# A decoder block on one core: when rests of weights are taken, in which order GLA's and FOX's first blocks run, and how the second norm is interleaved

## The chip, the cores and the metric

The kernel runs on 1 core of one Trainium2 chip. The metric is the device time of one execution in microseconds (us), the median of several runs. Lower is better.

## What is computed

One layer of a decoder block, 256 tokens by 2048 channels, all in float32:

```python
mod = silu(c) @ w_ada + b_ada                      # shift1, scale1, gate1, shift2, scale2, gate2
h = rms_norm(x, g_norm1) * (1 + scale1) + shift1
proj = h @ w_in                                    # 16416 columns: gq gk gv gg ga_low | fq fk fv f_logit | gate_a gate_b
o_a = rms_norm(gla(gq, gk, gv, log_a)) * silu(gg)  # gated linear attention, 4 heads
o_b = forgetting_attention(fq, fk, fv, log_f)      # FOX: causal softmax with a forget bias, 16 heads
merged = sig(gate_a) * (o_a @ w_proj_gla) + sig(gate_b) * (o_b @ w_proj_fox)
x = x + gate1 * (merged @ w_out)
h2 = rms_norm(x, g_norm2) * (1 + scale2) + shift2
x = x + gate2 * (relu(h2 @ w_ff1) ** 2 @ w_ff2)
out = rms_norm(x)
```

## The kernel before, in words

**Blocks and units.** Each product with a weight is cut into blocks of 512 output columns (a name such as `("fq", 1)`: FOX's queries, second block), and each block into 8 units of 256 rows of the weight. `NAME` (line 45) is the order of the blocks, and unit g is the g-th unit of the program: 0 to 23 the head (`gg`, `gv`, `fq`, first blocks, taken in two halves of h's channels), 24 to 119 the FOX blocks, 120 to 191 GLA's, 192 to 319 the gates and projections, 320 to 351 the output product, 352 to 607 the feed-forward. `("qk", 0)` holds GLA's first 256 query columns and first 256 key columns side by side, so its units are loaded by two DMAs with rows of 1 KB each; all other units are one DMA with rows of 2 KB. Both move 512 KB.

**Precision.** A product is computed in three passes of the float32r format: each weight unit is split into a top part (`whi`, by ScalarE, `hi(g)`, line 716) and a rest (`wlo` = weight minus top, by VectorE, `lo(g)`, line 1195). `h` is split in the same way (`hT`). `token_unit` (line 1801 and on, the matmul's line is 1817) runs the 12 matmuls of a unit and first waits for `lo(g)`. There are 4 buffers for the split weights, so `hi(g)` waits until TensorE has finished unit g-4, and 5 buffers for the loaded ones (`raw`), shared by the units and the rides.

**Rides.** The vector `mod` is also computed on the way. Its parts that the first norm needs come in 64 pieces of 512 KB (`first`, loop over `PIECES`), each multiplied into an accumulator by VectorE (line 1167); the others ride along with the units: `RIDE_AT` says at which unit g a ride (a 512 KB load of `w_ada`, rows of 4 KB, and one VectorE multiply-add, line 1313) is done, and `MOD_AT` at which unit TensorE sums a finished one. `ride_all` (line 162) writes these places; its last lines step g by 5, 2 or 3 units. The loads of units and rides go in one order (`STREAM`) through SyncE's queue, each after the buffer five places earlier is free.

**The ramp.** While the pieces run, SyncE loads unit g at piece `LOAD_AT[g]`, VectorE takes its rest by piece `SPLIT`, and TensorE runs it by piece `RUN`. At piece 32, VectorE also makes h's second half of channels (`norm1_chunk(1)`). After piece 63, `sum_first(3)` on TensorE, `mod_first(3)` on VectorE and `shift_hi`, `shift_lo` complete h. The head and units 24 and 25 run during the ramp; from unit 26 the loop over FOX follows, where u counts the 24 units of one `it`.

**The turn.** FOX needs queries and keys transposed. ScalarE copies a finished block from PSUM to `fqk_tok` (`stage`, line 739), TensorE transposes it with 8 small matmuls (`turn`, line 1801), and ScalarE copies the result out (`take_turned`, line 747). For `("fq", 0)`, ScalarE stages at u = 5, after `hi` of the unit 3 ahead, and TensorE turns at u = 7, ahead of unit 31. For `("qk", 0)`, they stand at u = 8 (stage), 10 (turn) and 11; for `("fk", 0)` at 16, 18 and 19. All engines run their instructions strictly in the order in which they are written. `small` (16 + 16 narrow columns of `w_in`) is loaded by GpSimd's queue in 16 small DMAs from unit 21 on, and multiplied at u = 11 (`small_cols`, lines 1856 and 1858).

**The second norm** begins in the first units of the feed-forward, which run on the not yet shifted h2 (`obT`) for the first up block. Per channel tile k: `norm2_apply` (VectorE, line 1588) scales xT, `norm2_hi` (ScalarE, line 1043) makes its top, `norm2_lo` (VectorE, line 1594) its rest. VectorE's round u does `lo(g+3)`, then apply for two tiles, then `norm2_lo` for the two tiles of the round before; ScalarE's round u does `hi(g+3)`, then `norm2_hi` for two tiles. At u = 8 VectorE finishes the first up block (`ff_first`, lines 1642 and 1646), TensorE turns it at u = 11, and ScalarE and VectorE split the result at u = 12.

Of the kernel before, what the change touches and what calls it, by code (L numbers as in the profile page):

```python
# [13 lines left out]
KT = D // P  # L14
# [24 lines left out]
HEAD = [("gg", 0), ("gv", 0), ("fq", 0)]  # L39
FOX = [("qk", 0), ("fk", 0), ("fv", 0)] + [(what, it) for it in range(1, 4) for what in ("fq", "fk", "fv")]  # L40
GLA = [(what, it) for it in range(1, 4) for what in ("qk", "gg", "gv")]
# [63 lines left out]
LOAD_AT = [13, 14, 15] + [17 + 7 * _i // 4 for _i in range(9)] + [32] + [33 + 2 * _i for _i in range(1, 12)] + [57, 59, 61]  # L105
FOX_EARLY = 2
LOADED, SPLIT, RUN = [0] * PIECES, [0] * PIECES, [0] * PIECES
for _g, _p in enumerate(LOAD_AT):
    for _r in range(_p, PIECES):
        LOADED[_r] = _g + 1  # L110
    for _r in range(max(_p + 2, KT), PIECES):
        SPLIT[_r] = _g + 1
    if _g < G_FOX + FOX_EARLY:
        for _r in range(max(LOAD_AT[_g | 1] + 3, KT + 1), PIECES):
            RUN[_r] = _g + 1
# [18 lines left out]
UP_FROM = G_MIX + 34  # L134
# [25 lines left out]
def ride_all():  # L160
# [4 lines left out]
    while m < 6:  # L165
        if G_FOX + 24 <= g and j < SHIFTS and (n % 2 == 0 or g < free) or \
                UP_FROM <= g and SHIFTS <= j < UP_SHIFTS and (n % 3 == 0 or g < free):
            RIDE_AT[g] = ("w", j)
            j += 1
            if j == SHIFTS:  # L170
                SHIFT_AT[g + 4], SHIFT_AT[g + 6] = 1, 2
            if j == UP_SHIFTS:
                SHIFT_AT[g + 5] = 3
        elif g >= free:
            RIDE_AT[g] = ("a", (m, k))
            k += 1
            if k == KT:
                at = g + 4
                while any(a in SHIFT_AT for a in (at, at + 2)):
                    at += 1  # L180
                free = sums_at(m, at)
                m, k = m + 1, 0
        n += 1
        g += 5 if g < 43 else 2 if g < G_GLA or g >= UP_FROM else 3 if g < G_MIX or n % 2 else 2
    assert j == UP_SHIFTS and not set(SHIFT_AT) & set(MOD_AT)
    return free


_g = max(ride_all(), G_OUT - 5)

# [42 lines left out]
def build(nc, x, c, w_ada, b_ada, g_norm1, w_in, w_gla_a_up, b_gla_a, g_gla_out, b_fox_f,  # L233
# [299 lines left out]
    with nc.Block() as block:  # L533
# [138 lines left out]
        def _(act):  # L672
# [80 lines left out]
            def fox_stage(it, u):  # L753
# [4 lines left out]
                if u == 8:  # L758
                    stage(("fq", it) if it else ("qk", 0), fqk_tok)
                if u == 11:  # L760
                    if it:
                        act.wait_ge(s_qk, 4 * it)
                        take_turned(("fq", it), ((fq, FSC),))
                    else:
                        take_turned(("qk", 0), ((gq[0], GSC), (gk[0], 1.0)))
                if u == 16:
                    stage(("fk", it), fqk_tok)
                if u == 19:
                    take_turned(("fk", it), ((fk, 1.0),))

# [308 lines left out]
            for it in range(4):  # L1079
                for u in range(64):  # L1080
# [11 lines left out]
                    if u in (8, 16, 24, 32) and 4 * it + u // 8 > 1:  # L1092
                        relu(4 * it + u // 8 - 1)
                    if u in (12, 20, 28, 36):
                        ff_hi(4 * it + u // 8 - 1)
# [12 lines left out]
        def _(dve):  # L1108
# [487 lines left out]

            def norm2(u):

# [5 lines left out]
                if u == 1:  # L1604
                    for k in range(12, KT):
                        x2_lo(k)
                if u == 3:
                    dve.wait_ge(s_rrow, 1)
# [64 lines left out]
            for it in range(4):  # L1673
                for u in range(64):
                    g = G_FF + 64 * it + u
                    for n in ahead(g):
                        lo(n)
                    mod(g)
                    if it == 0 and u < 12:
                        norm2(u)  # L1680
                    if u == 0 and it:
                        residual(("down", 4 * it - 1), gate2, 3)
                    if u in (8, 16, 24, 32):
                        ff_sq(4 * it + u // 8 - 1)
                    if u in (12, 20, 28, 36):
                        ff_lo(4 * it + u // 8 - 1)
# [21 lines left out]
        def _(pe):  # L1708
# [294 lines left out]
            for it in range(4):  # L2003
                for u in range(24):
# [4 lines left out]
                    else:  # L2009
# [8 lines left out]
                        if u == 20:  # L2018
                            decay_sums()
                    if it == 0 and u == 7:  # L2020
                        turn(("fq", 0), fqk_tok)
                    if u == 10:
                        turn(("fq", it) if it else ("qk", 0), fqk_tok)
                    if u == 18:
                        turn(("fk", it), fqk_tok)
                    if u < 8:
                        ready = (lambda kt, hl: pe.wait_ge(s_hl if hl else s_hh, KT + kt + 1)) if it == 0 else None
                        if it or u >= FOX_EARLY:
                            token_unit(("fq", it) if it else ("qk", 0), u, hT, ready)
                    elif u < 16:  # L2030
                        token_unit(("fk", it), u - 8, hT)
                    else:
# [80 lines left out]
            for it in range(4):  # L2113
                for u in range(64):
# [42 lines left out]
```

## Time and profile before

| | |
|---|---|
| median of 3 runs | 1865.07 us (1863.8 to 1866.28) |
| profiled execution, its own time | 1863.37 us |
| its span, first to last instruction | 1861.6 us |
| TensorE busy (matmul) | 1826.9 us, 98% |
| VectorE, ScalarE, GpSimd busy | 1250.1, 851.6, 32.7 us |
| mean granted TensorE clock | 0.992 of full speed |
| DMA | 445.72 MB, mean 239 GB/s |

The own time of the profiled execution lies 1.77 us above its span and 1.70 us below the median of the three runs. A unit's 12 matmuls take 2.72 us when TensorE is fed; in a view that writes "x24" two units stand together.

### The profile page before, as it was taken

How to read it: one execution, taken by the hardware profiler on the slowest of the kernel's cores; microseconds unless marked ns; L12 is line 12 of the kernel's file. 1: busy time of each engine (PE TensorE's matmuls, PEld its weight loads, DVE VectorE, ACT ScalarE, POOL GpSimd, SP SyncE). 2: the span in 40 equal slices, each digit the busy share in tenths (PEclk: the TensorE clock that was granted, in tenths of full speed). 3: DMA queues.
4: the chain of work that ended last, by engine and by line, in shares of the span. 5: the costliest groups of instructions: out<-in, count | busy, mean ns of one | idle time of the engine just before them, and what ended most of it. 6: DMA issues, size and time to landing. Idle time of an engine off the chain costs nothing.

```text
span 1861.6 us, 21801 instructions
## 1 busy us (share of the span) xinstructions
PE 1826.9 (98%) x8353; PEld 1485.3 (80%) x8353; DVE 1250.1 (67%) x1402; ACT 851.6 (46%) x1089; POOL 32.7 (2%) x60
## 2 busy tenths in 40 slices
PE   6999999999999999999999999999999999999998
PEld 3667888888888888888888888788888888888886
DVE  5997667676666667667766787876555555555555
ACT  4445555455544554334444455443444344434443
POOL 1011000000000000000000000000000000000000
PEclk8999999999999999999999999999999999999999
DMA  9998898899997987999999786787666666666663
GB/s 382 401 338 245 214 229 279 245 236 252 208 209 248 211 249 238 251 272 308 332 258 273 270 274 216 229 276 229 191 186 189 193 191 182 192 193 192 183 191 124
DMA packets 213329, 445.72 MB, mean 239 GB/s; under 512 B 14693, under 2 KB 31429, under 8 KB 212842
## 3 DMA queue, kind: packets, MB, share of 16 engines
q1 hardware_dynamic: 211320, 440.51, 79.4%
q10 hardware_dynamic: 1138, 3.50, 0.5%
q8 instruction: 67, 1.10, 0.2%
q0 software_dynamic: 768, 0.31, 0.2%
q14 instruction: 36, 0.29, 0.0%
HBM read 442.12 MB, written 2.10 MB: 239 GB/s over the span
## 4 chain that ended last, share of the span: by engine, by line
PE 89%; DVE 1%; issue 1%; ACT 1%; DMA 0%; ACTq 0%; POOLq 0%; POOL 0%; DVEq 0%
PE ps L1817 83%; PE ps L1801 1%; PE ps L1921 1%; DVE wlo L1195 0%; PE ps L1973 0%; DMA raw<-in_w_in 0%; PE ps L1727 0%; PE ps L1725 0%; ACT whi L716 0%; PE ps L1930 0%; PE ps L2068 0%; PE ps L1856 0%; PE ps L1869 0%; PE ps L1943 0%; PE ps L1944 0%
## 5 line engine op out<-in xcount | busy, mean ns | idle before, releaser
L1195 DVE TENSOR_TENSOR wlo<-raw,whi 128x1024 fp32r<-128x1024 f32 x604 | 738.4, 1224 | 551.8 <-ACT whi L716 548.8
L716 ACT ACTIVATE whi<-raw 128x1024 fp32r<-128x1024 f32 x604 | 639.2, 1059 | 914.5 <-PE ps L1817 638.6
L1817 PE MATMUL ps<-whi,hT 128*128 128x512 f32 x3264 | 1042.9, 396 | 4.0 <-DVE wlo L1195 3.8
L1817 PEld LDWEIGHTS ps<-whi,hT 128*128 128x128 f32 x3264 | 616.3, 189 | 148.8 <-issue 11.1
L1817 PE MATMUL ps<-wlo,hT 128*128 128x512 f32 x1632 | 638.0, 391 | 0.0
L1817 PE MATMUL ps<-whi,oaT 128*128 128x512 f32 x1248 | 390.6, 391 | 0.0
L1817 PEld LDWEIGHTS ps<-wlo,hT 128*128 128x128 f32 x1632 | 308.6, 189 | 63.8 <-issue 1.9
L1817 PEld LDWEIGHTS ps<-whi,oaT 128*128 128x128 f32 x1248 | 234.3, 188 | 49.5 <-issue 1.2
L1817 PE MATMUL ps<-wlo,oaT 128*128 128x512 f32 x624 | 242.9, 389 | 0.0
L1313 DVE SCALAR_TENSOR_TENSOR acc<-raw,cond,acc 128x1024 f32<-128x1024 f32 x120 | 153.3, 1278 | 0.2
L1817 PEld LDWEIGHTS ps<-wlo,oaT 128*128 128x128 f32 x624 | 117.2, 188 | 25.2 <-issue 1.2
L1817 PE MATMUL ps<-whi,obT 128*128 128x512 f32 x320 | 101.6, 393 | 0.0
L1817 PEld LDWEIGHTS ps<-whi,obT 128*128 128x128 f32 x320 | 60.1, 188 | 12.9 <-issue 0.5
L1167 DVE SCALAR_TENSOR_TENSOR acch<-first,cond,acch 128x1024 f32<-128x1024 f32 (+1 forms) x60 | 64.2, 1070 | 8.4 <-DMA first<-in_w_ada 5.1
L1817 PE MATMUL ps<-wlo,obT 128*128 128x512 f32 x160 | 62.3, 389 | 0.0
L1817 PEld LDWEIGHTS ps<-wlo,obT 128*128 128x128 f32 x160 | 30.1, 188 | 6.5 <-issue 0.5
L1571 DVE TENSOR_TENSOR rt<-ps,gate 128x512 f32<-128x512 f32 x40 | 27.4, 684 | 8.1 <-PE ps L1817 8.1
L1575 DVE TENSOR_TENSOR xl<-xl,rt 128x512 f32<-128x512 f32 x40 | 27.7, 693 | 4.5 <-DVE rt L1571 0.5
L1775 PE MATMUL ps<-first,cond 128*1 128x512 f32 x48 | 27.0, 666 | 3.3 <-DMA first<-in_w_ada 3.3
L1661 DVE TENSOR_TENSOR oaT<-ps,oaT 128x512 fp32r<-128x512 f32 x32 | 20.5, 682 | 0.0
L1801 PE MATMUL ps<-ident,t 128*128 128x128 f32 x128 | 17.1, 276 | 2.3 <-DVE t L1646 2.3
L1655 DVE TENSOR_TENSOR t<-t 128x512 f32<-128x512 f32 x30 | 19.3, 684 | 0.0
(247 smaller groups left out, 825.7 us busy)
## 6 DMA issues: line engine op xcount, KB each, us to landing
raw<-in_w_ff SPq DMA_DIRECT2D x264, 512.0 KB, 4.2
raw<-in_w_in SPq DMA_DIRECT2D x248, 512.0 KB, 7.1
raw<-in_w_ada SPq DMA_DIRECT2D x128, 512.0 KB, 5.8
first<-in_w_ada SPq DMA_DIRECT2D x64, 512.0 KB, 10.1
raw<-in_w_in SPq DMA_DIRECT2D x64, 256.0 KB, 6.2
raw<-in_w_proj_fox SPq DMA_DIRECT2D x32, 512.0 KB, 5.6
raw<-in_w_proj_gla SPq DMA_DIRECT2D x32, 512.0 KB, 5.4
raw<-in_w_out SPq DMA_DIRECT2D x32, 512.0 KB, 5.5
```

The lines of the kernel that those rows point to most:

```text
L716: nc.scalar.activation(parts(g)[0][:], raw[POS_G[g] % RING][:], ACT.Copy).then_inc(s_hi, 1)
L1167: V.scalar_tensor_tensor(b[:, c], a[:, c], cond[:, k:k + 1], bih[:] if k == 0 else b[:, c], ALU.mult, ALU.add).then_inc(s_ada, 2)
L1195: V.tensor_tensor(rest[:], raw[POS_G[g] % RING][:], top[:].bitcast(F32), ALU.subtract).then_inc(s_lo, 1)
L1313: V.scalar_tensor_tensor(acc[:], raw[pos % RING][:].rearrange("p k n -> p (k n)"), cond[:, k:k + 1], acc[:], ALU.mult, ALU.add).then_inc(s ...
L1571: V.tensor_tensor(rt[:, t, :], ps[bank(name, t)][:], gate[:, cols], ALU.mult).then_inc(s_bk[bank(name, t)], 1)
L1575: V.tensor_tensor(xl[:, t, cols], xl[:, t, cols], rt[:, t, :], ALU.add).then_inc(s_x2, 1)
L1655: V.tensor_tensor(t5[:, t, :], t5[:, t, :], t5[:, t, :], ALU.mult).then_inc(s_act, 1)
L1661: V.tensor_tensor(oaT[:, 4 * b:4 * b + 4, 1, t * P:t * P + P], ps[bank(("up", n), t)][:].rearrange("p (k n) -> p k n", k=4), oaT[:, 4 * b: ...
L1775: T.matmul(ps[6][0:1, :], cond[:, k:k + 1], first[p % FRING][:, 0:NB], start=(p == p0), stop=(p == p1)).then_inc(s_adp, 1)
L1801: i = T.transpose(ps[bank(name, t)][:, k * P:k * P + P], src[:, t, k * P:k * P + P], ident[:])
L1817: i = T.matmul(ps[bank(name, t)][:], src[:, kt, hl, tk], w[:, k, :], start=(kt == 0 and n == 0), stop=(kt == KT - 1 and n == 2))
L1921: i = T.matmul(ps[4][:, c0:c0 + keys], fq[:, j, b * P:b * P + P], fk[:, j, 0:keys], start=False, stop=True, skip_group_check=True)
```

## The change

Four edits, and one in the order of the rides:

1. In the ramp, the rests of units 14, 15 and 16 are taken at pieces 32, 34 and 37 in place of 39, 41 and 43 (`CHUNK_SPLIT`). As `SPLIT` only grows, unit 13's moves from piece 37 to 32 with them.
2. The FOX stage starts with `("fk", 0)`, units 24 to 31, and `("qk", 0)` follows as units 32 to 39. Stage, turn and take of the two change places with them.
3. `("fq", 0)` is turned at u = 8, after unit 31, in place of u = 7, ahead of it. ScalarE's stage of it stays at u = 5.
4. In the second norm, VectorE's round is now apply, then `lo(g+3)`, then `norm2_lo` for the same two tiles. The finish of the first up block moves from u = 8 to 9, its turn from 11 to 12, its split from 12 to 13.
5. `ride_all` steps by 2 and 3 units in turn between units 120 and 226, in place of 3 and 3 (to unit 192), then 3 and 2. The rides from unit 121 on move: those of the sixth of the eight sums end at unit 306 in place of 314. Up to unit 151 there are two more of them than before (at 123, 126, 128, 131, 133, 138, 141, 143, 146, 148, 151 in place of 124, 127, 130, 133, 136, 142, 145, 148, 151). The rides from unit 320 on are where they were.

```diff
-FOX = [("qk", 0), ("fk", 0), ("fv", 0)] + [(what, it) for it in range(1, 4) for what in ("fq", "fk", "fv")]
+FOX = [("fk", 0), ("qk", 0), ("fv", 0)] + [(what, it) for it in range(1, 4) for what in ("fq", "fk", "fv")]
...
+CHUNK_SPLIT = {14: 32, 15: 34, 16: 37}
...
     for _r in range(max(_p + 2, KT), PIECES):
         SPLIT[_r] = _g + 1
+        if _r == max(_p + 2, KT) and _g in CHUNK_SPLIT:
+            for _q in range(CHUNK_SPLIT[_g], _r):
+                SPLIT[_q] = _g + 1
...
-        g += 5 if g < 43 else 2 if g < G_GLA or g >= UP_FROM else 3 if g < G_MIX or n % 2 else 2
+        g += 5 if g < 43 else 2 if g < G_GLA or g >= UP_FROM or n % 2 else 3
...
-_g = max(ride_all(), G_OUT - 5)
+_g = max(ride_all(), G_OUT)
...
                 if u == 8:
-                    stage(("fq", it) if it else ("qk", 0), fqk_tok)
+                    stage(("fq", it) if it else ("fk", 0), fqk_tok)
...
+                if u == 16:
+                    stage(("fk", it) if it else ("qk", 0), fqk_tok)
+                if u == 19:
+                    if it:
+                        take_turned(("fk", it), ((fk, 1.0),))
+                    else:
                         take_turned(("qk", 0), ((gq[0], GSC), (gk[0], 1.0)))
...
-            def norm2(u):
+            def norm2_early(u):
+
+                if u == 3:
+                    dve.wait_ge(s_rrow, 1)
+                if 3 <= u < 11:
+                    for k in (2 * (u - 3), 2 * (u - 3) + 1):
+                        norm2_apply(k)
+
+            def norm2_late(u):
...
                 if 3 <= u < 11:
                     for k in (2 * (u - 3), 2 * (u - 3) + 1):
-                        norm2_apply(k)
-                if 4 <= u < 12:
-                    for k in (2 * (u - 4), 2 * (u - 4) + 1):
                         norm2_lo(k)
...
+                    if it == 0:
+                        norm2_early(u)
                     for n in ahead(g):
                         lo(n)
                     mod(g)
-                    if it == 0 and u < 12:
-                        norm2(u)
+                    if it == 0:
+                        norm2_late(u)
...
-                    if u in (8, 16, 24, 32):
+                    if u in (16, 24, 32) or u == (8 if it else 9):
                         ff_sq(4 * it + u // 8 - 1)
...
-                    if it == 0 and u == 7:
+                    if it == 0 and u == 8:
                         turn(("fq", 0), fqk_tok)
...
-                    if u in (11, 19, 27, 35):
+                    if u in (19, 27, 35) or u == (11 if it else 12):
                         turn(("up", 4 * it + u // 8 - 1), t5)
```

## Rows read from the trace of the kernel before

**Rows 1.** The page, busy time and share of the span by engine.
```profile
PE 1826.9 (98%) x8353; PEld 1485.3 (80%) x8353; DVE 1250.1 (67%) x1402; ACT 851.6 (46%) x1089; POOL 32.7 (2%) x60
```

**Rows 2.** What TensorE waited for: total us, times, longest.
```profile
PE ps L1801 <- ACT fqk_tok L739: 2.7, 1, 2.7
PE ps L1801 <- DVE t L1646: 2.3, 1, 2.3
```

**Rows 3.** The chain that ended last, 147 to 168 us: start, duration, what.
```profile
147.26 7.38 DMA raw<-in_w_in
...
155.63 0.59 ACT fqk_tok L739
...
156.26 1.97 PE ps L1801 x8
158.23 8.91 PE ps L1817 x36
167.14 0.87 PE ps L1801 x8
```

**Rows 4.** The same chain in the feed-forward.
```profile
1165.76 1.55 PE ps L1801 x8
1167.32 6.76 PE ps L1817 x24
...
1174.93 5.49 PE ps L1817 x24
```

**Rows 5.** TensorE's timeline, the last matmul ahead of each of the two waits.
```profile
153.18 0.39 PE L1817 MATMUL ps<-whi,hT 128*128 128x512 f32 x1
...
1163.03 0.39 PE L1817 MATMUL ps<-whi,hT 128*128 128x512 f32 x1
```

**Rows 6.** VectorE's timeline in the second norm; in brackets idle time before and releaser.
```profile
1160.99 1.22 DVE L1195 TENSOR_TENSOR wlo<-raw,whi 128x1024 fp32r<-128x1024 f32 x1 [0.75 <-ACT whi L716]
1162.13 0.87 DVE L1588 SCALAR_TENSOR_TENSOR xT<-xT,gcol,ps 128x256 f32<-128x256 f32 x2
1162.91 0.87 DVE L1594 SCALAR_TENSOR_TENSOR hT<-xT,modc,hT 128x256 fp32r<-128x256 f32 x2
1163.71 1.40 DVE L1642 SCALAR_TENSOR_TENSOR t<-ps,nst,up 128x512 f32<-128x512 f32 x2
1165.03 1.28 DVE L1646 SCALAR_TENSOR_TENSOR t<-t 128x512 f32<-128x512 f32 x2
```

**Rows 7.** ScalarE's timeline at the entry of FOX.
```profile
154.67 1.06 ACT L716 ACTIVATE whi<-raw 128x1024 fp32r<-128x1024 f32 x1 [1.83 <-DMA raw<-in_w_in]
...
161.79 1.06 ACT L716 ACTIVATE whi<-raw 128x1024 fp32r<-128x1024 f32 x1 [2.17 <-PE ps L1817]
...
163.71 1.09 ACT L739 ACTIVATE fqk_tok<-ps 128x512 f32<-128x512 f32 x2
```

**Rows 8.** VectorE's timeline there: the rest of unit 31.
```profile
152.87 1.23 DVE L1195 TENSOR_TENSOR wlo<-raw,whi 128x1024 fp32r<-128x1024 f32 x1 [2.68 <-ACT whi L716]
```

**Rows 9.** Windows: stretch, length, busy us (instructions) by engine, TensorE clock, DMA share, GB/s.
```profile
80.00:95.00 15.00, 12.26 (x41) 7.72 (x40) 14.20 (x14) 7.00 (x12) 0.00 (x0) 0.89 1.04 402
130.00:145.00 15.00, 14.58 (x63) 11.07 (x62) 12.65 (x19) 6.70 (x12) 4.82 (x7) 0.89 0.92 214
145.00:150.00 5.00, 5.00 (x23) 4.13 (x22) 4.65 (x6) 1.69 (x2) 4.13 (x3) 1.00 0.93 167
147.00:165.00 18.00, 15.31 (x65) 12.57 (x65) 12.36 (x14) 8.79 (x13) 2.84 (x2) 0.91 0.98 294
460.00:490.00 30.00, 30.00 (x156) 25.55 (x155) 21.83 (x36) 18.47 (x39) 0.00 (x0) 1.00 0.95 210
490.00:520.00 30.00, 30.00 (x175) 25.20 (x174) 18.46 (x23) 15.23 (x22) 0.00 (x0) 1.00 0.95 195
520.00:550.00 30.00, 30.00 (x132) 23.91 (x132) 20.94 (x28) 12.99 (x17) 1.16 (x1) 1.00 0.98 224
```

**Rows 10.** Unit 152: VectorE takes its rest.
```profile
551.68 1.23 DVE L1195 TENSOR_TENSOR wlo<-raw,whi 128x1024 fp32r<-128x1024 f32 x1 [1.52 <-ACT whi L716]
```

**Rows 11.** Unit 152: its last matmul on TensorE.
```profile
556.40 0.39 PE L1817 MATMUL ps<-whi,hT 128*128 128x512 f32 x1
```

**Rows 12.** The ramp: TensorE at unit 13.
```profile
87.65 0.54 PE L1817 MATMUL ps<-whi,hT 128*128 128x512 f32 x1 [2.74 <-DVE wlo L1195]
```

**Rows 13.** The ramp: VectorE at the last piece.
```profile
134.69 1.29 DVE L1167 SCALAR_TENSOR_TENSOR acch<-first,cond,acch 128x1024 f32<-128x1024 f32 x1
```

More of the change, by code:

```diff
@@ L764, in fox_stage @@
                     else:
+                        take_turned(("fk", 0), ((fk, 1.0),))
+                if u == 16:
[4 more added lines that the diff above has]
+                    else:
                         take_turned(("qk", 0), ((gq[0], GSC), (gk[0], 1.0)))
[L766 to L769, printed above, removed]
             def shift_silu(g):
@@ L1093, in _ @@
                         relu(4 * it + u // 8 - 1)
-                    if u in (12, 20, 28, 36):
+                    if u in (20, 28, 36) or u == (12 if it else 13):
                         ff_hi(4 * it + u // 8 - 1)
@@ L1606, in norm2 @@
                         x2_lo(k)
-                if u == 3:
-                    dve.wait_ge(s_rrow, 1)
                 if 3 <= u < 11:
                     for k in (2 * (u - 3), 2 * (u - 3) + 1):
-                        norm2_apply(k)
-                if 4 <= u < 12:
-                    for k in (2 * (u - 4), 2 * (u - 4) + 1):
                         norm2_lo(k)
@@ L1678, in _ @@
                     mod(g)
-                    if it == 0 and u < 12:
-                        norm2(u)
+                    if it == 0:
+                        norm2_late(u)
                     if u == 0 and it:
                         residual(("down", 4 * it - 1), gate2, 3)
-                    if u in (8, 16, 24, 32):
+                    if u in (16, 24, 32) or u == (8 if it else 9):
                         ff_sq(4 * it + u // 8 - 1)
-                    if u in (12, 20, 28, 36):
+                    if u in (20, 28, 36) or u == (12 if it else 13):
                         ff_lo(4 * it + u // 8 - 1)
@@ L2019, in _ @@
                             decay_sums()
-                    if it == 0 and u == 7:
+                    if it == 0 and u == 8:
                         turn(("fq", 0), fqk_tok)
                     if u == 10:
-                        turn(("fq", it) if it else ("qk", 0), fqk_tok)
+                        turn(("fq", it) if it else ("fk", 0), fqk_tok)
                     if u == 18:
-                        turn(("fk", it), fqk_tok)
+                        turn(("fk", it) if it else ("qk", 0), fqk_tok)
                     if u < 8:
@@ L2028, in _ @@
                         if it or u >= FOX_EARLY:
-                            token_unit(("fq", it) if it else ("qk", 0), u, hT, ready)
+                            token_unit(("fq", it) if it else ("fk", 0), u, hT, ready)
                     elif u < 16:
-                        token_unit(("fk", it), u - 8, hT)
+                        token_unit(("fk", it) if it else ("qk", 0), u - 8, hT)
                     else:
```

## The prediction, made before the result was known

> **What bounds the kernel now.** The page first: TensorE's matmuls cover 98% of the span [rows 1], so only what makes TensorE wait or run slowly can be won back. The list of its waits names two that this change can touch: 2.7 us ahead of a turn for ScalarE's stage of FOX's first queries, and 2.3 us ahead of the turn of the first up block for VectorE [rows 2]. Then I followed the chain of waits at both places. At the first, a load that lands after 7.38 us releases ScalarE, which converts it and only then stages; the turn follows [rows 3]. At the second, VectorE's squares release the turn [rows 4]. Last I looked for what the change could newly uncover: DMA share by stretch [rows 9], and how far ahead of TensorE the rest of a unit is [rows 10, 11].
>
> **What each stall really costs.** A turn's 8 matmuls take 0.87 us when TensorE is fed [rows 3], two units 5.49 us [rows 4], so a unit's matmuls start 0.23 us apart. Second place: the last matmul ahead of it starts at 1163.03 [rows 5], so TensorE is free at 1163.26 and idle to 1165.76 (2.50 us); the turn takes 1.55 us, 0.68 too many, and the next two units 6.76, 1.27 too many [rows 4]. Sum: 4.5 us. First place: free at 153.41 [rows 5], idle to 156.26 (2.85); turn 1.97, 1.10 too many; the next three units 8.91 against 8.24, 0.67 too many [rows 3]. Sum: 4.6 us. The slow matmuls after each wait are at the lower of the clock's two levels, 1.2 GHz instead of 2.4: about twice the time each, after 2 to 3 us of idleness.
>
> **Second norm.** Before, VectorE's round is a ping-pong: its `lo` waits 0.75 us for ScalarE's `hi` [rows 6], which stands behind the two `norm2_hi` that wait for VectorE's apply. `lo` 1.14, apply 0.79, `norm2_lo` 0.79 (starts in rows 6) and the waits make 3.55 us, against 2.72 for TensorE's unit. After, apply comes first, ScalarE works during `lo`, and `norm2_lo` finds its top finished: 1.14 + 0.79 + 0.79 = 2.72 us a round, at TensorE's pace. The apply of u = 8 stood at 1162.13, so the first, five rounds earlier, at about 1144.4, and it stays there. Seven new rounds (u = 3 to 9) end at 1144.4 + 19.1 = 1163.5; there the finish begins, as before at 1163.71, and its first squares are there 2.0 us later (1163.71 to 1165.76 before [rows 4, 6]), so at 1165.5. TensorE, one unit later, wants them at 1163.26 + 2.72 = 1165.98. The stall goes, 0.5 us to spare: **-4.5 us**. What comes late next: `lo` of unit 365, delayed by the finish (2.5 us), is done about 1168.2, needed at 1169.6. ScalarE's `ff_hi` and VectorE's `ff_lo` one unit later are needed only at the third up block. Nothing of this moves a DMA except that `lo` frees raw buffers sooner.
>
> **Entry of FOX.** The turn of the queries now stands behind unit 31: TensorE goes on at 153.41 with that unit if its rest is there, and turns at 156.13. Even with the old landing the first half is staged at 156.22 (155.63 + 0.59 [rows 3]), so the move alone hides it. The rest of unit 31 was ready only at 154.10 [rows 8], 0.7 us late; but as an fk unit its 512 KB come in 2 KB rows. DMA moved 214 GB/s at a share of 0.92 in the stretch of 1 KB loads (2.25 us per load) and 294 at 0.98 in that of fk (1.75 us) [rows 9]; in the first stretch the small loads also ran. Three or four faster loads bring unit 31's rest to about 152.2. So up to 4.6 us are won by here.
>
> Against it: the slow loads are now units 32 to 35. What is queued behind them is ScalarE's round u = 8: `hi(35)`, take of the queries, stage of the keys. Before, `hi(35)` started at 161.79 and waited for TensorE, not for the load, and the stage started 1.92 us later [rows 7]; its first half is ready 2.55 us after `hi(35)` begins. TensorE wants it at 153.41 + 2.72 + 0.87 + 5.45 = 162.45, so load 35 must land by 159.9. Working the queue forward from load 31's landing (about 149): one ride (1.3 us at the 402 GB/s of rows 9), then loads 32 and 33 (2.25 each), one shift load (1.75), loads 34 and 35, give 161.1. At 1.75 us for each it would be 159.1: no wait. I take 2.25, the stretch with the same row size, so a wait of **1.2 us**; bounds 0 and 5 (load 31 landing 2 us later, plus some 1.7 us of slow clock as at the first place). Net **-3.4 us**. The Trainium skill, in "DMA: Bandwidth & Descriptors", section "Why small descriptors are slow (HBM only)", puts a fixed overhead of some 3 cycles on each packet beside one cycle per 32 bytes: by it 1 KB rows cost only about 4% more than 2 KB rows. By that rule the wait would be gone and the net -4.6; the trace of the 1 KB stretch shows more than that, but with other traffic beside it, so it doesn't decide.
>
> **Rides.** Two more rides lie ahead of unit 152. From 460 to 550 us the DMA share is 0.95 to 0.98 at only 195 to 224 GB/s [rows 9]: the queue, not TensorE, paces the loads. Unit 152's rest is ready at 551.68 + 1.23 = 552.91, TensorE starts it 2.49 us ahead of its last matmul at 556.40, so at 553.91 [rows 10, 11]: 1.0 us to spare. A ride costs the queue between 1.3 us (402 GB/s) and 2.7 us (195 GB/s). Taking 1.3, for 4 KB rows of the same tensor made that 402, two cost 2.6; the 5% free in 460 to 490 is 1.5 us and absorbs as much. Left: 2.6 - 1.5 - 1.0 = 0.1, and by the full price 5.4 - 1.0 = 4.4. I put **+0.6 us**, near the low end, as rides and pieces are rows of the same kind. In the later stretches the count changes by one ride at most, with one less ahead of unit 232, and the sums (`MOD_AT`) only move: nothing for them here, the rest in rival C.
>
> **Ramp.** The earlier rests relieve TensorE at unit 13, where it waited 2.74 us [rows 12]. But VectorE ends the ramp with the last piece (134.69 + 1.29 [rows 13]) and is the loaded engine from there on (14.20 of 15 us at 80 to 95, [rows 9]); it does the same work in another order. TensorE just waits later. SyncE's loads behind these rests are issued earlier, into a queue already full at 402 GB/s [rows 9]. **0**, bounds -0.5 and +1 (a longer idle time ahead of the next sum).
>
> **Sum.** -4.5 - 3.4 + 0.6 = -7.3. The profiled execution (1863.37) goes to 1856.1, the median, 1.70 above it, to **1857.8 us**. A measurement of this kernel tells 0.2%, 3.7 us, from no change.
>
> **Rivals.**
> *A. The 1 KB loads cost no more than the others*: no wait at the keys' turn, -4.5 - 4.6 + 0.6 = -8.5, 1856.6. For it: the 214 GB/s were measured beside the small loads, which are through before most of the qk loads now. Against: a share of 0.92, so a queue that was hardly idle. Chance 0.15. The rule of the Trainium skill named above would give this case.
> *B. The wait at the queries' turn moves to the keys'* and eats FOX's gain, 3.4 + 1.2 wait plus slow clock: -3.9, 1861.2. For it: ScalarE's fixed order, `hi(35)` ahead of the stage. Against: it needs load 35 to land near 163. Chance 0.12.
> *C. The denser rides stall TensorE* at units 151 to 153 by the full price, 4.4 us, with 1.6 us slow clock: -7.3 - 0.6 + 6.0 = -1.9, 1863.2. Chance 0.09.
> *D. The second norm does not get faster*: if ScalarE still ties the round to 3.55 us, the later finish meets the later turn with the same wait: -7.3 + 4.5 = -2.8, 1862.3. Against: the arithmetic above has ScalarE at 1.9 us a round. Chance 0.07.
> *E. Slower: the load queue becomes the bound at both places.* From 145 to 150 us it moved only 167 GB/s [rows 9], 3.1 us per load. If that belongs to these columns, not to the small loads beside them, the four qk loads end 3.5 us later: wait 4.7 + 1.6 clock; with C's 6.0 the balance is -4.5 - 4.6 + 6.3 + 6.0 = +3.2, 1868.3. It decides from 2.3 us per qk load if the rides stall as in C (-9.1 + 6.0 + 1.2 + 1.6 + 4 x 0.08 = 0), and without that only from 3.7. Against: it takes the ends of two unknowns at once. Chance 0.05.
>
> My forecast, a fall of 5.5 to 8.5 us, has 0.52. Range: best sum -9.5 with a little spread of medians, 1854.8, to C, 1863.2. Faster by over 0.2%: forecast, A, half of B and a little of C and D, 0.78; within 0.2%: 0.17; slower: 0.05.
>
> **What would show it.** TensorE's waits should lose both rows of rows 2; the chain should pass from unit 30 through 31 to the turn at about 156; in VectorE's timeline of the norm the 0.75 us idle before `lo` should be gone and rounds 2.7 us apart. A new wait "ACT fqk_tok" near 162 is my 1.2 us; one of over 3 is B. A wait for `wlo` near 545 to 552 us is the rides'. I am wrong if the ramp ends anywhere but at 136, or if the norm's turn still waits.

## The result and the profile after

| | before | after |
|---|---|---|
| median | 1865.07 us (7 runs, 1863.8 to 1868.26) | 1870.23 us (7 runs, 1869.28 to 1872.68) |
| profiled execution: own time, span | 1863.37, 1861.6 us | 1870.23, 1868.5 us |

The ratio is 1.0026, 95% interval 1.0017 to 1.0036: the changed kernel is slower, by 3 to 7 us. The forecast was 1857.8 (1854.8 to 1863.2), so it was wrong in size and in sign.

The page of the changed kernel hardly moves, busy times first and then the chain's shares by engine:

```profile
PE 1828.2 (98%) x8353; PEld 1483.6 (79%) x8353; DVE 1249.0 (67%) x1402; ACT 851.6 (46%) x1089; POOL 30.8 (2%) x60
...
PE 83%; DMA 5%; DVE 2%; issue 1%; ACT 1%; SPq 0%; ACTq 0%; POOLq 0%; POOL 0%; DVEq 0%
```

TensorE's waits in it (total us, times, longest) answer to [rows 2]. Line numbers are a few higher: the turn is L1813, was L1801; a unit's matmuls are L1829, were L1817.

```profile
PE ps L1829 <- DVE wlo L1202: 8.8, 11, 3.9
PE ps L1813 <- ACT fqk_tok L743: 5.7, 1, 5.7
PE ps L1797 <- DVE acch L1174: 4.5, 2, 4.2
```

The wait of the norm's turn for VectorE (2.3 us) is gone, as forecast. The wait ahead of a turn at FOX's entry hasn't gone: it is 5.7 us instead of 2.7. And the waits for a unit's rest (`wlo`) are 8.8 us in 11 places; in the kernel before their row was this:

```profile
PE ps L1817 <- DVE wlo L1195: 3.8, 4, 2.7
```

**Where the time went, unit by unit.** The start of a unit's first matmul, from TensorE's timeline of both traces, tells how late the changed kernel stands. Only units with the same number of modulation sums ahead of them are compared, since a moved sum alone shifts a start.

| unit | before | after | difference | what lies since the row above |
|---|---|---|---|---|
| 30 | 150.69 | 151.47 | +0.78 | ramp |
| 31 | 157.88 | 154.19 | -3.69 | turn of the queries, without its wait |
| 34 | 167.77 | 171.52 | +3.75 | turn of the keys |
| 40 | 193.84 | 200.42 | +6.58 | two low-clock stretches |
| 200 | 699.47 | 706.53 | +7.06 | rides ahead of unit 152 |
| 321 | 1043.99 | 1055.23 | +11.24 | late feed of w_in loads |
| 400 | 1274.55 | 1281.46 | +6.91 | second norm |

The difference at unit 31 flatters the change, since the turn of the queries (0.87 us when fed) now comes behind it. At unit 32 both kernels have turned: 161.53 before, 157.94 after, so 4.4 us were won from unit 30 to there. The first steps came as forecast: TensorE goes straight from unit 30 into 31, and turns the queries at 157.05 without a wait. Then the keys' turn. TensorE's timeline of the changed kernel, its last matmul of unit 33, the turn and the first of unit 34:

```profile
163.83 0.39 PE L1829 MATMUL ps<-whi,hT 128*128 128x512 f32 x1
169.90 1.97 PE L1813 MATMUL ps<-ident,fqk_tok 128*128 128x128 f32 x8 [5.69 <-ACT fqk_tok L743]
171.52 0.78 PE L1829 MATMUL ps<-whi,hT 128*128 128x512 f32 x1
```

The turn waits for ScalarE's stage of FOX's keys. ScalarE's timeline says why (the highs of units 33, 34 and 35, take, stage):

```profile
158.82 1.06 ACT L720 ACTIVATE whi<-raw 128x1024 fp32r<-128x1024 f32 x1 [1.34 <-DMA raw<-in_w_in]
163.50 1.06 ACT L720 ACTIVATE whi<-raw 128x1024 fp32r<-128x1024 f32 x1 [3.62 <-DMA raw<-in_w_in]
167.33 1.06 ACT L720 ACTIVATE whi<-raw 128x1024 fp32r<-128x1024 f32 x1 [2.78 <-DMA raw<-in_w_in]
168.30 1.07 ACT L751 ACTIVATE fq<-ps 128x512 f32<-128x512 f32 x2
169.25 1.09 ACT L743 ACTIVATE fqk_tok<-ps 128x512 f32<-128x512 f32 x2
```

Load 35 lands at 167.3; 161.1 was forecast, 159.9 was needed. The chain of waits passes through it, issue and transfer:

```profile
153.08 1.98 SPq L586
155.11 1.32 SPq L586
156.47 10.84 DMA raw<-in_w_in
```

After 5.7 us of idleness TensorE runs at the lower of its two clock levels, 1.2 GHz (granted clock 0.50 from 170.0 to 173.8 us): the turn takes 1.97 us for 0.87 and unit 34's twelve matmuls 3.87 for 2.72. A second slow stretch follows at unit 37, without an idle gap in the profile (granted clock 1.00 from 186.5 to 190, 0.66 from 190 to 195 us). TensorE's timeline has the eight matmuls of the decay ahead of it, the unit's first matmul and a later pair at the low clock, 1.06 us for two instead of 0.62:

```profile
186.56 3.70 PE L1881 MATMUL ps<-wup,gl 17*128 17x512 f32 x8
190.19 0.50 PE L1829 MATMUL ps<-whi,hT 128*128 128x512 f32 x1
...
192.94 1.06 PE L1829 MATMUL ps<-whi,hT 128*128 128x512 f32 x2
```

**The second norm** came out to the letter. VectorE's round in the changed kernel, apply, rest, low part, and the next apply, which answer to [rows 6]:

```profile
1166.46 0.86 DVE L1595 SCALAR_TENSOR_TENSOR xT<-xT,gcol,ps 128x256 f32<-128x256 f32 x2
1167.24 1.22 DVE L1202 TENSOR_TENSOR wlo<-raw,whi 128x1024 fp32r<-128x1024 f32 x1
1168.38 0.88 DVE L1601 SCALAR_TENSOR_TENSOR hT<-xT,modc,hT 128x256 fp32r<-128x256 f32 x2
1169.17 0.87 DVE L1595 SCALAR_TENSOR_TENSOR xT<-xT,gcol,ps 128x256 f32<-128x256 f32 x2
```

A round is 2.71 us, no idle time in brackets. The chain has the turn between two runs of matmuls with nothing waited for, and at full clock; it answers to [rows 4]:

```profile
1159.89 17.46 PE ps L1829 x77
1177.36 0.87 PE ps L1813 x8
1178.23 2.77 PE ps L1829 x12
```

**Two losses without a term in the forecast.** The ramp: TensorE is early at units 13 to 16, then idles 3.90 us ahead of unit 17, whose rest comes when it did before, and runs that unit at the low clock (granted clock 0.60 from 101.6 to 105.9 us). And late in the token part, units 288 to 321: the same bytes flow, but TensorE is busy for 97.04 of 100 us, and from 955 to 1055 us ScalarE waits 36.5 us in all for w_in loads:

```profile
930.00:1030.00 100.00, 97.04 (x417) 77.46 (x417) 65.49 (x58) 39.25 (x41) 0.00 (x0) 1.00 0.93 264
```

### The profile page after: what moved, and what is told of

It is laid out like the page before. It is cut to its first block, busy times and chain, and to the rows that moved or that the text cites. A ratio compares the mean times of both kernels' runs of the same rounds, so it can differ in the third digit from the quotient of the medians.

```text
span 1868.5 us, 21801 instructions
## 1 busy us (share of the span) xinstructions
PE 1828.2 (98%) x8353; PEld 1483.6 (79%) x8353; DVE 1249.0 (67%) x1402; ACT 851.6 (46%) x1089; POOL 30.8 (2%) x60
## 4 chain that ended last, share of the span: by engine, by line
PE 83%; DMA 5%; DVE 2%; issue 1%; ACT 1%; SPq 0%; ACTq 0%; POOLq 0%; POOL 0%; DVEq 0%
PE ps L1829 77%; DMA raw<-in_w_in 4%; PE ps L1813 1%; ACT whi L720 1%; PE ps L1933 1%; DMA raw<-in_w_proj_fox 1%; DVE acc L1320 1%; DVE wlo L1202 1%; SPq L586 0%; PE ps L1985 0%; DMA raw<-in_w_proj_gla 0%; PE ps L1737 0%; PE ps L1739 0%; PE ps L1942 0%; PE ps L1868 0%
## 5 line engine op out<-in xcount | busy, mean ns | idle before, releaser
L1829 PE MATMUL ps<-whi,hT 128*128 128x512 f32 x3264 | 1045.4, 396 | 9.2 <-DVE wlo L1202 8.8
L1829 PEld LDWEIGHTS ps<-whi,hT 128*128 128x128 f32 x3264 | 616.0, 189 | 157.9 <-DVE wlo L1202 20.2
L1829 PE MATMUL ps<-wlo,hT 128*128 128x512 f32 x1632 | 638.2, 391 | 0.0
L1829 PE MATMUL ps<-whi,oaT 128*128 128x512 f32 x1248 | 389.6, 391 | 0.0
L1829 PEld LDWEIGHTS ps<-wlo,hT 128*128 128x128 f32 x1632 | 308.3, 189 | 64.1 <-issue 2.4
L1829 PEld LDWEIGHTS ps<-whi,oaT 128*128 128x128 f32 x1248 | 234.2, 188 | 49.1 <-issue 0.7
L1829 PE MATMUL ps<-wlo,oaT 128*128 128x512 f32 x624 | 242.8, 389 | 0.0
L1829 PEld LDWEIGHTS ps<-wlo,oaT 128*128 128x128 f32 x624 | 117.2, 188 | 24.8 <-issue 0.7
L1829 PE MATMUL ps<-whi,obT 128*128 128x512 f32 x320 | 100.7, 391 | 0.0
L1829 PEld LDWEIGHTS ps<-whi,obT 128*128 128x128 f32 x320 | 60.1, 188 | 12.7 <-issue 0.2
L1829 PE MATMUL ps<-wlo,obT 128*128 128x512 f32 x160 | 62.3, 389 | 0.0
L1829 PEld LDWEIGHTS ps<-wlo,obT 128*128 128x128 f32 x160 | 30.0, 188 | 6.3 <-issue 0.2
L1268 DVE SCALAR_TENSOR_TENSOR accv<-raw,modc,accv 128x1024 f32<-128x1024 f32 x15 | 19.1, 1275 | 0.0
```

What stands on the lines that cost most here:

```text
L1268: V.scalar_tensor_tensor(acc_, w, col, acc_, ALU.mult, ALU.add).then_inc(s_wacc, inc)
L1829: i = T.matmul(ps[bank(name, t)][:], src[:, kt, hl, tk], w[:, k, :], start=(kt == 0 and n == 0), stop=(kt == KT - 1 and n == 2))
```

## The experiments

Every time is the median of its runs; the ratio is to the kernel before, run on the same chip in turn with it. The interval of a ratio is 0.0008 to 0.0010 to either side (e4: 0.0015); 0.001 is 1.9 us.

### Each edit undone, and the others alone

e1, the swap undone (stages, takes and turns of the pair go back with it):

```diff
-FOX = [("fk", 0), ("qk", 0), ("fv", 0)] + [(what, it) for it in range(1, 4) for what in ("fq", "fk", "fv")]
+FOX = [("qk", 0), ("fk", 0), ("fv", 0)] + [(what, it) for it in range(1, 4) for what in ("fq", "fk", "fv")]
```

> The changed kernel with one of its edits undone: GLA's first queries and keys are loaded, split and multiplied ahead of FOX's first keys again, as before; the later turn of FOX's queries, the second norm, the rests behind h's second chunk and the new order of the rides stay. Theory K (the keys' turn): the swap put the staging of FOX's keys on ScalarE behind the split of load 35, so that TensorE idles 5.7 us at the keys' turn and then runs twice at the low clock; taking the swap back gives all of that back (about 10 us from the lead of 3.7 to 4.4 us that TensorE has at unit 31 to the lag of 6.6 us at unit 40), and the later turn's gain of 2 to 4.6 us stays: before 1865.1, less 4.5 of the norm, less 2 to 4.6, plus 0.75 of the ramp, plus 4.6 of the rides late in the feed-forward gives 1861 to 1864 us. Rival L (the loads): the stretch loses its time because the load queue is full there, whatever comes first; then taking the swap back leaves at least half of the loss, and the time is 1866 us or more.

Measured: 1862.48 us, ratio 0.9981. From 1.0026 that is 8.4 us (0.0045 x 1865). Its trace has no wait above 0.5 us ahead of any turn:

```profile
PE ps L1826 <- DVE wlo L1199: 9.4, 11, 3.9
...
PE ps L1810 <- ACT fqk_tok L743: 0.5, 1, 0.5
```

Theory K holds: the swap is the edit that costs. But the 11 waits for `wlo` stay, so they don't come from the swap.

e2, the old order of the rides:

```diff
-        g += 5 if g < 43 else 2 if g < G_GLA or g >= UP_FROM or n % 2 else 3
+        g += 5 if g < 43 else 2 if g < G_GLA or g >= UP_FROM else 3 if g < G_MIX or n % 2 else 2
-_g = max(ride_all(), G_OUT)
+_g = max(ride_all(), G_OUT - 5)
```

> The changed kernel with the order of the rides (which sums of the modulation are taken between which units) as before; everything else as changed. Theory R: the 4.6 us that the changed kernel loses between units 288 and 321 come from two more rides just ahead of the slow stretch of w_in loads, so with the old order they come back, and the entry of FOX keeps its loss: 1870.2 less 4.6, 1865 to 1866.5 us. Rival: that loss is the later start of TensorE against loads that it meets in another phase, whatever the rides; then the time stays within 1.5 us of 1870.

Measured: 1866.54 us, ratio 1.0005, 3.9 us less than with the new order, at the edge of what was expected. The loss between units 200 and 321 falls from 4.2 to 1.9 us; the keys' turn waits 5.4 us as in the changed kernel. Theory R holds in the main: the medians give back nearly all of its 4.6 us (4.2 in the table above), this trace half.

e3, the rests where they were:

```diff
-CHUNK_SPLIT = {14: 32, 15: 34, 16: 37}
+CHUNK_SPLIT = {}
```

> The changed kernel with the rests of the first chunks split where they were before (directly behind their own high parts, not behind h's second chunk). Theory: the edit brings unit 13 forward by 3.3 us, but TensorE then idles 3.9 us ahead of unit 17, whose last rest comes when it did before, and runs that unit at the low clock, so the edit costs 0.75 us and undoing it gives them back: 1869.5 us. Rival: the edit is worth the time between the earlier units 13 to 16, and undoing it costs 1 us or more.

Measured: 1868.8 us, ratio 1.0014. Unit 30 starts at 150.97 instead of 151.47. The edit costs 0.5 us by this trace and 2.2 by the ratios, whose intervals overlap; the table of all traces below says more.

e4, the kernel before with the later turn and the new norm only:

```diff
-                    if it == 0 and u == 7:
+                    if it == 0 and u == 8:
                         turn(("fq", 0), fqk_tok)
```

(and the norm's part of the change as it is)

> The kernel before with only two edits: the turn of FOX's first queries later, and the second norm in its new order. GLA's first queries and keys stay ahead of FOX's first keys, the rides and the rests stay as before. Theory: the norm gives 4.5 us, as the trace of the changed kernel shows between units 321 and 364, and the later turn takes away the wait of 2.3 us and the low clock behind it, up to 4.6 us: 1856 to 1858.5 us. Rival: the later turn only moves the wait, since hi of the next load stands behind it on ScalarE: 1860 to 1861 us.

Measured: 1859.64 us, ratio 0.9962, interval 0.9947 to 0.9977. It beats both kernels, by 7 us the one before (0.0038 x 1865) and by 12 the changed one, but it misses the 1856 to 1858.5 expected. Its trace has no wait ahead of the turn, so the rival (the wait only moves) doesn't explain the miss; unit 31 waits 0.43 us for its rest, and unit 37 runs at the low clock.

e5, the kernel before with the norm's part only:

> The kernel before with one edit: the second norm in its new order. Theory: 4.45 us between units 321 and 364 and nothing elsewhere, 1861 us where before has 1865 to 1866; the kernel with the later turn of FOX's first queries as well stood at 1859.6, so the later turn would be worth the 1 to 2 us between them. Its trace also shows the kernel before a second time up to unit 321: if TensorE waits about 2 us around unit 311 here too, as it does in every kernel with an edit and did not in the trace of the kernel before, that loss belongs to no edit. Rival: units 306 to 321 run through without those waits, as in the kernel before, and the loss comes with a TensorE that arrives there at another time.

Measured: 1860.10 us, ratio 0.9980, so 3.7 us; its trace gives 4.42 between units 321 and 364. The later turn is then worth 3.4 us by the ratios of e4 and e5, though their intervals overlap a little. Their traces, counted from unit 30, have 3.0 us at unit 34 and 1.4 at unit 40, where e4 has lost 1.6 to the low clock of unit 37. Units 288 to 321 ran through here (0.3 us lost). A new thing showed: up to unit 30 this kernel does the work of the kernel before, yet its unit 30 came 2.2 us later, since the sum that ends the ramp waited for VectorE. TensorE's timeline there:

```profile
138.34 1.95 PE L1794 MATMUL ps<-ones,acch 128*128 128x1 f32 x16 [2.52 <-DVE acch L1171]
```

Before, that wait was 0.33 us. The trace the forecast rests on was a lucky one at this place: e4 and e11, alike there, have 1.78 and 1.04 us of it, and all three come to unit 30 between 2.0 and 2.2 us later.

### Inside the entry: ScalarE's order, or the loads?

e6, take and stage ahead of the high part of unit 35:

```diff
-                if u == 8:
-                    stage(("fq", it) if it else ("fk", 0), fqk_tok)
+                if u == 8 and it:
+                    stage(("fq", it), fqk_tok)
...
+                    if it == 0 and u == 8:
+                        take_turned(("fq", 0), ((fq, FSC),))
+                        stage(("fk", 0), fqk_tok)
                     if it or u:
                         hi(G_FOX + 24 * it + u + LEAD)
...
-                    if it == 0 and u == 8:
-                        take_turned(("fq", 0), ((fq, FSC),))
```

> The changed kernel with ScalarE's round at unit 34 in another order: FOX's first queries are taken and FOX's first keys staged for their turn ahead of the split of load 35, not behind it. Theory K (in-order ScalarE): the staging waited for a load that it does not need; TensorE's wait of 5.7 us at the keys' turn shrinks to under 2 us and the low clock of unit 34 goes with it; unit 34 starts at 166 to 167.5 instead of 171.5, and the time is 1865 to 1867 us. Rival L (the load itself): unit 35 or 36 then waits for the split of load 35, which landed at 167.3 and only now comes behind the staging, so that the wait moves and the time stays at 1869 us or more.

Measured: 1866.93 us, ratio 1.0014, 2.2 us less than the changed kernel, though the intervals overlap. The wait falls to 3.2 us, not under 2, and unit 34 starts at 169.07, not by 167.5:

```profile
PE ps L1814 <- ACT fqk_tok L743: 3.2, 1, 3.2
```

ScalarE's timeline of e6 shows what is left: now the stage stands behind the high part of unit 34, whose load landed at 164.9.

```profile
164.97 1.06 ACT L720 ACTIVATE whi<-raw 128x1024 fp32r<-128x1024 f32 x1 [4.98 <-DMA raw<-in_w_in]
165.93 1.06 ACT L751 ACTIVATE fq<-ps 128x512 f32<-128x512 f32 x2
166.89 1.08 ACT L743 ACTIVATE fqk_tok<-ps 128x512 f32<-128x512 f32 x2
```

ScalarE's order is part of the mechanism (2.9 us from unit 30 to 34 in the traces); one place further up the next late load takes over. So the loads themselves were tried.

e7, one transfer with rows of 2 KB; e9, the same rows but two transfers for each load:

```diff
-    _loads = 2 if _kind == "g" and UNITS[_what][0][0] == "qk" else 1
+    _loads = 2 if _kind == "g" and UNITS[_what][0][0] == "qk" and UNITS[_what][0][1] else 1
...
+        if what == "qk" and it == 0:
+            return [w_in_v[:, ks, C_GQ:C_GQ + NB]]
         if what == "qk":
```

```diff
+        if what == "qk" and it == 0:
+            return [w_in_v[:, KU * u + a:KU * u + a + 1, C_GQ:C_GQ + NB] for a in range(KU)]
         if what == "qk":
...
-                        sp.dma_start(r[:, :, a * n:a * n + n], src).then_inc(s_raw[pos % RING], 16)
+                        tall = kind == "g" and UNITS[what][0] == ("qk", 0)
+                        sp.dma_start(r[:, a:a + 1, :] if tall else r[:, :, a * n:a * n + n],
+                                     src).then_inc(s_raw[pos % RING], 16)
```

Both edits change two things of these loads at once: the length of a row, and which columns of `w_in` are read (512 columns side by side, in place of 256 of the queries and 256 of the keys, which lie apart).

> The changed kernel with each load of GLA's first queries and keys made as one transfer with rows of 2 KB instead of two with rows of 1 KB. It leaves out GLA's first key columns: in their place the columns beside the queries are loaded, so block 0's keys hold other numbers. Same bytes, half the packets, one issue instead of two. Theory W (small rows): loads 32 to 39 land 1 to 3 us earlier each, load 35 by 164.5 instead of 167.3, the wait at the keys' turn falls from 5.7 to about 3 us or less, and the time is 1865 to 1867.5 us. Rival Q (the queue): the stretch is bound by the bytes that are asked for there, and load 35 lands within 1 us of 167.3 with either rows; the time stays within 1 us of 1870.

> As the run with rows of 2 KB (it leaves out GLA's first key columns in the same way), but each of those loads is two transfers again, one per row of a partition: the issues and the bytes are as in the changed kernel, only the rows are 2 KB instead of 1 KB. Theory W (row size): it behaves as with one transfer, with no wait at the keys' turn, 1863 to 1865 us. Rival I (issues): SP's second issue of each load is the cost (the chain of the changed kernel has 2.0 and 1.3 us of SP's issues), and the wait of 5 to 6 us and about 1868 to 1870 us come back.

Measured: e7 1863.69 us, ratio 1.0002; e9 1864.78 us, ratio 1.0000. In both traces the wait at the keys' turn is gone altogether and unit 34 starts at 164.34 and 164.12, 3.4 and 3.6 us ahead of the kernel before, though they came to unit 30 0.9 to 1.1 us behind it: the entry gains 4.5 us, the 4.6 that the forecast had without its term for the wait. e7 comes out below the 1865 to 1867.5 expected of it, e9 within its 1863 to 1865. One stretch with the same loads queued, 147 to 165 us, shows it (DMA share and GB/s are the last two columns); the changed kernel first, then e9:

```profile
147.00:165.00 18.00, 16.95 (x77) 13.18 (x75) 11.15 (x13) 5.23 (x6) 3.62 (x3) 1.00 0.93 220
```

```profile
147.00:165.00 18.00, 18.00 (x89) 15.08 (x88) 14.60 (x17) 10.01 (x13) 3.71 (x3) 1.00 0.98 331
```

The queue is as busy in both and moves half as much again in e9. The groups of raw loads issued from 147 to 162 us (duration of an issue in ns, and time from issue to landing), the changed kernel and then e9:

```profile
L586 SPq DMA_DIRECT2D raw<-in_w_in x11: 367/1030/1980, 148.0 to 161.2; - x11
...
DMA to landing us min/median/max: 4.8/8.8/10.8
```

```profile
L588 SPq DMA_DIRECT2D raw<-in_w_in x14: 328/379/433, 148.3 to 160.9; - x14
...
DMA to landing us min/median/max: 3.6/4.8/5.6
```

Load by load it is plainer still. In the changed kernel's trace loads 32 to 35 land 3.3, 3.4, 3.4 and 3.8 us behind the load before each in the queue, a shift load with 2 KB rows between them 1.3; in e9 the same four land 1.3, 1.3, 1.3 and 1.9 us behind theirs. The number of issues is the same, so rival I falls (an issue itself takes longer when the queue is slow, 1.0 against 0.4 us): these loads, as they are laid out, are the cause.

That it is the length of their rows, theory W, is not shown. The changed kernel's own trace speaks against it as a rule. Two later stretches of its queue, packets and then windows: from 460 to 468 us it carries mostly 1 KB rows (GLA's second queries and keys), from 470 to 490 no 1 KB rows at all, only GLA's second `gg` block with 2 KB rows and some rides:

```profile
DMA packets 1918, 2.63 MB, mean 329 GB/s; under 512 B 127, under 2 KB 1662, under 8 KB 1917
...
DMA packets 1957, 4.29 MB, mean 215 GB/s; under 512 B 127, under 2 KB 127, under 8 KB 1955
```

```profile
460.00:468.00 8.00, 8.00 (x38) 6.71 (x37) 5.21 (x9) 6.19 (x13) 0.00 (x0) 1.00 0.98 329
470.00:490.00 20.00, 20.00 (x103) 17.00 (x102) 15.84 (x26) 13.15 (x29) 0.00 (x0) 1.00 0.99 215
```

In equally full queues the short rows are fast here and the long ones slow. The repetition (e12) has 332 and 213 GB/s in the same two stretches. So a load's price goes with the part of `w_in` that it reads at least as much as with its rows, and a run that changes the rows without the columns is missing.

By the medians the two edits are worth 4.5 to 4.8 us, less than the 8.7 us that their traces show from unit 30 to 40; e9's profiled execution is the fastest of its runs, so its trace flatters it, and both lose 4.7 to 6.0 us again between units 200 and 321. What takes back the rest was not found.

### The rides

e8, the changed kernel with the sixth sum's rides held back:

```diff
-        elif g >= free:
+        elif g >= free and (m < 5 or g >= 284):
```

> The changed kernel with the rides of the sixth sum held back until unit 284, where the old order had them, all other rides in the new order. Undoing the whole order of the rides took 2.3 us of the 4.2 us that the changed kernel loses between units 288 and 321, and 1.9 us stayed. Theory R (rides right ahead of the slow w_in loads): holding back two rides gives those 2.3 us, 1868 us. Rival V (this stretch varies from one execution to the next whatever the rides): the trace shows another loss there, anywhere from 0 to 5 us, and the median stays within 1 us of 1870.

Measured: 1867.37 us, ratio 1.0014, 2.2 us less, though the intervals overlap. The line holds back four rides (at units 276 to 282), not two, and the last four then come at 308 to 314. From 930 to 1030 us TensorE is busy throughout in its trace, at the same bytes:

```profile
930.00:1030.00 100.00, 100.00 (x446) 82.43 (x444) 66.17 (x60) 41.51 (x44) 0.00 (x0) 1.00 0.93 265
```

### All causes taken away, the best version, and the changed kernel again

e10 is e7 with e8's line and e3's; e11 is the changed kernel with e1's, e3's and e8's edits; e12 is the changed kernel unaltered.

> The changed kernel with rows of 2 KB in one transfer for GLA's first queries and keys (its first key columns left out as before in that run), the rides of the sixth sum held back until unit 284, and the rests of the first chunks where they were. All three causes that the earlier runs point to are taken away. If they add up, the change gives what was forecast of it: before 1864 to 1866, less 4.4 of the norm, less 3.4 to 4.2 of the entry, plus up to 1.6 of the low clock near unit 37, 1857 to 1859.5 us. Rival: they don't add up, since a TensorE that is ahead meets the next wait; then 1860.5 us or more.

> The kernel before with the later turn, the second norm and the new order of the rides, with the sixth sum's rides not before unit 284: no swap, rests as before. It is the version that the runs point to as the best. The same with the old order of the rides stood at 1859.6 us (ratio 0.9962) and lost 2.1 us at units 306 to 321 in its trace. If the held rides cover the slow loads better, that goes and the ratio is 0.995 to 0.9965; if the order of the rides is worth nothing, 0.996 to 0.997; if the new order costs elsewhere (unit 152), above 0.997.

> The changed kernel itself once more, for a second trace. What the experiments ascribe to an edit should be there again: a wait of 5 to 6.5 us at the keys' turn and unit 34 at 171 to 172, 3.5 to 5 us between units 288 and 321, the norm's 4.4 us; the ratio 1.002 to 1.0035. What differs between the two traces by more than 0.5 us at a place is chance of the execution: the low clock of unit 37 (present in some traces and not in others) is the candidate.

Measured: e10 1860.09 us, ratio 0.9972; e11 1859.72 us, ratio 0.9971; e12 1868.98 us, ratio 1.0025 (1.0017 to 1.0034). e10 gives 5.2 us of the 7.3 forecast; it lies between what was expected if the causes add up and what its rival gave, so that stays open. e11 doesn't beat e4 (their intervals overlap), so no gain of the new order of the rides is shown. e12 repeats the result and its places: wait 5.3 us at the keys' turn, unit 34 at 171.07, 3.5 us between 200 and 321 (2.9 of them behind unit 288, where 3.5 to 5 were expected), 4.45 at the norm. That makes 14 traces, and three places can be judged over them:

| place | with | without |
|---|---|---|
| units 200 to 321, us lost against the first trace | new rides (changed kernel, e1, e3, e6, e7, e9, e12): 4.2, 4.3, 6.4, 2.9, 6.0, 4.7, 3.5 (mean 4.6) | old rides (before, e2, e4, e5): 0, 1.9, 2.2, 0.3 (mean 1.1); held (e8, e10, e11): 0.3, 4.3, 2.7 (mean 2.4) |
| unit 30 against the first trace, keys first | new split: 0.8, 1.1, 1.3, 1.1, 0.8, 0.9, 1.0 | old split: 0.3, -0.2 |
| the same, GLA's first | new split: 1.8 | old split: 0, 2.2, 2.1, 2.0 |

So the rides cost about 3.5 us at that stretch, in which single executions differ by as much. The earlier rests cost about 0.9 us with FOX's keys first, over only two traces without them; with GLA's first, the one trace that has them stands no later than the usual execution.

## Why the prediction was wrong

- **Second norm, -4.5: right.** 4.45 us in the traces of the changed kernel and its repetition, 4.42 in e5 alone, with rounds of 2.71 us (forecast 2.72). Rival D is out.
- **Turn of the queries, up to -4.6: right.** From unit 30 to 32, with the turn behind it in both kernels, 4.4 us were won. By itself, ahead of GLA's queries and keys, the move is worth 3.4 us (e4 against e5).
- **The keys' turn, +1.2: the step that failed.** The mechanism was named (ScalarE's round u = 8 behind `hi(35)`), but the loads with 1 KB rows were priced at 2.25 us each, from a window that averaged 214 GB/s (2.45 us for 512 KB, scaled to a full queue) and held other loads too. They cost 3.3 to 3.8 us each (2.4 to 3.7 in e12), four of them 4.9 us more than assumed; the ride ahead of them landed 2.5 us behind load 31 instead of 1.3, and the shift load 1.3 instead of 1.75. With load 31 itself 0.6 late, load 35 came 6.2 us after the forecast. Rival E's price of 3.1 stood in the same [rows 9] (145 to 150 us), nearer to the truth, and I gave it to the small loads beside. The trace of the kernel before also had these very loads one by one: the last four landed 2.1, 4.7, 1.9 and 4.1 us behind the load ahead of each, 3.2 on average. The wait was 5.7 us, the turn 1.1 too long and unit 34 1.2: 8.0 us, past the bound of 5. From unit 30 to 35 the entry lost 4.2 us (4.97 - 0.78) where a gain of 3.4 was forecast. e1, e7 and e9 show that the late loads are the cause, e6 the share of ScalarE's order.
- **Rows and the rule.** Between e9 and the changed kernel the row's length and the columns read differ, and the queue moves 331 and 220 GB/s. That is against rival A: these loads do cost more than the others. The Trainium skill, "DMA: Bandwidth & Descriptors", section "Why small descriptors are slow (HBM only)", has some 3 cycles of overhead on a packet beside one cycle per 32 bytes, which would put some 4%, an estimate from those two figures, between rows of 1 and 2 KB. No run here tests that price, as none changes the rows alone; with 1 KB rows at 329 GB/s and 2 KB rows at 215 in one trace, the rows need not be what makes these loads slow.
- **Clock, no term.** The low-clock stretch at unit 37 is in 10 of 14 traces (1.6 us each, 3.2 in e10 and e11), not in those of before, e1, e2 and e5. The profile shows no idle gap ahead of it. What decides was not found.
- **Rides, +0.6: right ahead of unit 152, wrong after it.** There 0.5 us were lost, 0 in e12. "Nothing for them" in the later stretches failed: some 3.5 us around units 288 to 321 (e2, and the table). I had counted rides per stretch, not where they fall against the slow w_in loads, and one count was wrong: between units 152 and 200 the new order has three more, which cost nothing there (145.64 us against 145.56). That the rides just ahead of unit 284 are the cause is shown in part: holding them back took 2.2 us by the ratios, but one of its three traces lost 4.3.
- **Ramp, 0 with +1 as bound: within it.** +0.8 in the trace (its last sum starts at 136.78, 136.03 before), 0.9 against the old rests with this order. The edit also moves the rests of units 11 and 12 up to piece 32, from 33 and 34.
- **Rivals.** The outcome is E's: slower, by one of its two halves (the price of the loads, if anything too low) and a late form of C's rides at another place. It had 0.05, since I asked for both ends at once; the late stretch was in none of its terms. B had the right place, and its own price, a gain merely eaten up, was too small.

The sum by the differences of the table of units (the turn at unit 31, before its 0.87 us come): +0.8 ramp, -4.5 turn, +7.4 keys' turn, +2.8 slow clock after it, +0.5 rides, +4.2 late, -4.45 norm, +0.1 at the end = +6.9, the difference of the two spans (1868.5 - 1861.6).

## What to carry to other kernels

When a change moves a group of loads in front of a deadline, price them from single landings of those same loads in the trace before, not from the mean of a window that mixes them, and ask what stands behind them on every in-order engine: here ScalarE held a finished accumulation for a load it didn't need. Take each edit of a bundle alone before judging it: this one held a gain of 7 us (the turn and the norm, e4) and losses of 12. And one profiled execution is one draw: at the end of the ramp the trace before was 2 us better than three others of the same work.

## What the runs showed of the hardware

- What a full queue moves depends on what it reads, and not by row length alone. Loads of 512 KB of GLA's first queries and keys, in rows of 1 KB, landed 3.3 to 3.8 us behind the load before; 512 columns side by side from the queries on, in rows of 2 KB, 1.3 to 1.9 us (e9). But in the changed kernel's trace the queue moved 329 GB/s at a share of 0.98 with mostly 1 KB rows (460 to 468 us), and 215 at 0.99 with none (470 to 490 us).
- Whether a load of 2 KB rows was one transfer or two made no difference that could be measured (e7 1.0002, e9 1.0000).
- In the changed kernel TensorE's clock fell to its lower level at unit 17 after 3.9 us of idleness (granted clock 0.60 from 101.6 to 105.9 us), at unit 34 after 5.7 us (0.50 from 170.0 to 173.8), and at unit 37 without an idle gap in the profile, behind the decay's eight matmuls in 3.7 us (0.66 from 190 to 195); the last only in some executions of the same work.
- The same kernel before ranged from 1861.5 to 1869.9 us over 29 runs on one chip, so a difference of 0.2% could be told only over many runs of each.
